# Where the two seven-product units stand in a feed-forward chunk, and when the up product of the chunk before is combined

## The reference, cut to what matters

```python
def _swiglu_ffn(x, norm_g, w_gate, w_up, w_down):
    h = _rmsnorm(x, norm_g)
    return (jax.nn.silu(h @ w_gate) * (h @ w_up)) @ w_down
# h (256, 2048) f32, w_gate and w_up (2048, 5632) f32, w_down (5632, 2048) f32
```

## Time and profile before

| | us |
|---|---|
| median of 3 runs | 2634.55 (2633.47 to 2634.83) |
| the profiled execution | 2630.96 |
| its span | 2629.2 |
| TensorE busy (modelled ends) | 2591.3 (99%) |
| VectorE busy | 1778.8 (68%) |
| ScalarE busy | 1280.2 (49%) |
| granted TensorE clock, mean | 0.999 |

### The profile page before, as it was taken

One profiled execution on the slowest core, in us unless ns is written; L12 is line 12 of the kernel. 1 busy time (PEld: TensorE's weight loads), 2 busy tenths in 40 slices (PEclk: granted clock), 3 DMA queues, 4 the chain that ended last, 5 costly groups with the idle time before them and its releaser, 6 DMA issues.

```text
span 2629.2 us, 33942 instructions
## 1 busy us (share of the span) xinstructions
PE 2591.3 (99%) x13749; PEld 2119.6 (81%) x13749; DVE 1778.8 (68%) x2085; ACT 1280.2 (49%) x1494; POOL 188.7 (7%) x346
## 2 busy tenths in 40 slices
PE   8999999999999999999999999999999999999998
PEld 7887878888888787878788888888888777888887
DVE  6887886545566796958666756555668888855444
ACT  5545454444456365546455544433555455544443
POOL 2000000000000011010001112000100000000000
PEclk9999999999999999999999999999999999999999
DMA  7666667766666665656488879644767676776554
GB/s 226 213 220 210 223 214 225 225 208 208 207 207 184 193 209 170 183 156 185 149 277 262 250 241 288 195 148 141 235 193 230 202 230 207 232 227 224 193 195 157
DMA packets 278573, 548.20 MB, mean 209 GB/s; under 512 B 25020, under 2 KB 35424, under 8 KB 278032
## 3 DMA queue, kind: packets, MB, share of 16 engines
q1 hardware_dynamic: 253904, 478.60, 57.7%
q0 software_dynamic: 24192, 66.89, 8.7%
q10 hardware_dynamic: 320, 0.53, 0.1%
HBM read 508.15 MB, written 37.77 MB: 208 GB/s over the span
## 4 chain that ended last, share of the span: by engine, by line
PE 74%; DVE 14%; DMA 5%; issue 4%; ACT 3%; POOL 0%; SPq 0%; DVEq 0%; ACTq 0%; POOLq 0%
PE pp L367 19%; PE pp L369 18%; PE pp L368 18%; PE pp L803 4%; PE pp L802 4%; PE pp L801 4%; DMA raw<-in_ffn_w_up 3%; DVE wlo L892 3%; DVE wlo L328 2%; DVE tw L900 1%; ACT whi L323 1%; DVE hid L939 1%; DVE tw L907 1%; DVE tw L904 1%; DVE cb L936 1%
## 5 line engine op out<-in xcount | busy, mean ns | idle before, releaser
L328 DVE TENSOR_TENSOR wlo<-raw,whi 128x1024 fp32r<-128x1024 f32 (+1 forms) x824 | 998.6, 1218 | 647.6 <-ACT whi L323 635.1
L323 ACT ACTIVATE whi<-raw 128x1024 fp32r<-128x1024 f32 (+1 forms) x824 | 864.9, 1054 | 950.5 <-PE pp L369 817.9
L367 PE MATMUL pp<-whi,xhi 128*128 128x512 f32 (+1 forms) x1184 | 470.3, 397 | 0.7 <-DVE xlo L504 0.7
L369 PE MATMUL pp<-wlo,xhi 128*128 128x512 f32 (+1 forms) x1184 | 459.4, 388 | 0.0
L368 PE MATMUL pp<-whi,xlo 128*128 128x512 f32 (+1 forms) x1184 | 459.3, 388 | 0.0
L801 PE MATMUL pp<-whi,xhi 128*128 128x512 f32 x832 | 323.8, 389 | 0.0
L802 PE MATMUL pp<-whi,xlo 128*128 128x512 f32 x832 | 323.8, 389 | 0.0
L803 PE MATMUL pp<-wlo,xhi 128*128 128x512 f32 x832 | 323.7, 389 | 0.0
L367 PE MATMUL pp<-whi,hhi 128*128 128x512 f32 x688 | 267.6, 389 | 0.0
L368 PE MATMUL pp<-whi,hlo 128*128 128x512 f32 x688 | 267.6, 389 | 0.0
L369 PE MATMUL pp<-wlo,hhi 128*128 128x512 f32 x688 | 267.6, 389 | 0.0
(11 more groups left out here) (498 smaller groups left out, 3199.1 us busy)
## 6 DMA issues: line engine op xcount, KB each, us to landing
raw<-in_ffn_w_gate SPq DMA_DIRECT2D x176, 512.0 KB, 4.4
raw<-in_ffn_w_up SPq DMA_DIRECT2D x176, 512.0 KB, 4.7
raw<-in_ffn_w_down SPq DMA_DIRECT2D x176, 512.0 KB, 4.5
raw<-in_w_in SPq DMA_DIRECT2D x144, 512.0 KB, 4.4
hid_dram<-hid_t POOLq DMA_DIRECT2D x43, 512.0 KB, 3.3
xq<-hid_dram POOLq DMA_DIRECT2D x156, 128.0 KB, 4.8
raw<-in_w_lift SPq DMA_DIRECT2D x32, 512.0 KB, 5.6
raw<-in_w_out SPq DMA_DIRECT2D x32, 512.0 KB, 5.1
```

The source lines that it names most:

```text
L323: nc.scalar.activation(whi[:, s, :, 0:width], raw[:, r % RING, :, 0:width], ACT.Copy).then_inc(whi_ready, 1)
L328: nc.vector.tensor_tensor(wlo[:, s, :, 0:width], raw[:, r % RING, :, 0:width], whi[:, s, :, 0:width].bitcast(F32), ALU.subtract).then_inc( ...
L367: nc.tensor.matmul(out, a_hi[:, k0 + k, tok], w_hi, start=first, stop=False)
L369: mm = nc.tensor.matmul(out, a_hi[:, k0 + k, tok], w_lo, start=False, stop=final)
```

## The change

UNIT_AFTER becomes (1, 5): unit 0 goes behind plain slot 1, unit 1 stays behind plain slot 5. The gate goes plain 0, 1, unit 0, plain 2, 3, 4, 5, unit 1, on every engine and for the loads. On VectorE finish(i - 1) is called inside unit 0, after the third sum and before the split of slot w + 1, and no longer includes the transpose; nat_turn comes behind the split of plain slot 3. Outside the seven-product chunks gated_turned keeps the old order. The rest of the diff makes the closing flags of the accumulation depend on where the last unit stands, and adds a wait for the split of the token forms, whose memory tw shares, before the first sum of the first such chunk.

```diff
-UNIT_AFTER = (3, 5)
+UNIT_AFTER = (1, 5)
...
+            unit_last = UNIT_AFTER[-1] == PLAIN - 1
...
-                        mm = product(out, xhi[:, k, tok], xlo[:, k, tok], n % RING, kk, k == 0 and opened, pr is up and k == PLAIN * SK - 1)
+                        mm = product(out, xhi[:, k, tok], xlo[:, k, tok], n % RING, kk, k == 0 and opened, k == PLAIN * SK - 1 and (pr is up or not unit_last))
...
-                product(e11, *x(1, A_FIRST), w % RING, 1, False, final).then_inc(slot_used, 1)
+                product(e11, *x(1, A_FIRST), w % RING, 1, False, final and unit_last).then_inc(slot_used, 1)
...
-                product(e21, *x(1, A_SECOND), (w + 3) % RING, 1, False, final).then_inc(slot_used, 1)
+                product(e21, *x(1, A_SECOND), (w + 3) % RING, 1, False, final and unit_last).then_inc(slot_used, 1)
...
-            def unit(w, r, u):
+            def unit(w, r, u, between=None):
...
                 dve.wait_ge(*loaded(r + 1))
+                if i == SEVEN[0] and u == 0:
+                    dve.wait_ge(sem("banks_free"), forms_split(tag))
...
                 v.tensor_tensor(tw[:, 2, :], tw[:, 0, :], blocks[:, b22, :], ALU.add).then_inc(sem("sums_ready"), 1)
+                if between is not None:
+                    between()
                 lo(w + 1, wlo[:, (w + 1) % RING, :, :], tw[:, 0:2, :], whi[:, (w + 1) % RING, :, :])
...
                 if j == 3:
-                    finish(i - 1)
+                    nat_turn(dve, None, nats[tag + "act"] + i - 1)
                 if j in UNIT_AFTER:
-                    unit(*gate["units"][UNIT_AFTER.index(j)])
+                    u = UNIT_AFTER.index(j)
+                    unit(*gate["units"][u], between=(lambda: finish(i - 1)) if u == 0 else None)
...
             op.then_inc(nat_ready, 1)
-            nat_turn(dve, None, nats[tag + "act"] + i)
...
+            def gated_turned(i):
+                gated(i)
                 nat_turn(dve, None, nats[tag + "act"] + i)
...
                         if j == 4:
-                            gated(i - 1)
+                            gated_turned(i - 1)
...
                     if c == 0 and j == 3:
-                        gated(NFC - 1)
+                        gated_turned(NFC - 1)
```

## The result

The changed kernel takes 2612.57 us (median of 4, 2609.87 to 2613.76) where the kernel before takes 2634.14 in runs beside it: 21.6 us less, ratio 0.9917, 95% interval 0.9903 to 0.9930. In a later session with more runs it was 2614.67 against 2632.74, ratio 0.9927 (0.9914 to 0.9940).

What follows compares the result with a forecast made beforehand. TensorE bounds the seven-product chunks, with 20.9 us idle; the whole loss less half a microsecond for small gaps, -20.4, takes the 2634.55 us median to 2614.2, range 2613 to 2622 (chance 0.84).

Steps and rivals of the forecast that it cites:

- The bound: Sixteen seven-product chunks: TensorE loses 20.9 us, 1.3 per chunk, in gaps at the second unit.
- The added wait, flags, e12, the transpose's way to xq: Banks wait, stop flags, TensorE product awaiting unit 0's combination, later store and reload of the hidden chunk: all cost 0.
- Unit 1: Second unit's loads get earlier-released buffers, land by 15.5 us into the chunk, bound 17.5; all gaps go, -20.9 us.
- 17.38: Latest start, in us after the chunk's first matmul, of unit 1's 7.11 us chain that opens no gap.
- Rival 1: Second unit keeps a gap, its loads taking 6.8 us beside store and reload: gain 15.3, 2619.3 us; chance 0.13.
- two signs named in the prediction: Unit 1's first sum without idle time before it; up loads' waits in ScalarE gone.
- Unit 0: First unit, wanted 5.44 us earlier: its later load lands at -1.2 to -2.2; zero gap, by 0.2 to 1.2 us.
- S: Start of unit 0's first sum against its chunk's first matmul; may be up to -0.97 without a gap.
- Rival 3: Slower: unit 0 starts on a late load with 2.70 us more work inside; 36 lost less 20.9, 2650 us; chance 0.08.
- The rule on HBM latency: Skill page's 2 us at high load would run unit 0 dry 0.8 to 1.8 us, around 2635 to 2640; rows preferred.
- a gain over 21: Sign: a gain over 21 us would mean time was lost outside the seven-product chunks, unseen by the prediction.
- transpose moved behind p3: VectorE's 1.25 us transpose moves from 5 to about 10.7 into the chunk, reload to 15.4; later reads stay covered.

Runs made afterwards that it cites:

- sum_repeated2: Changed kernel with unit 0's first sum done three times in place of once; 2638.91 us, ratio 1.0016 against the kernel before.
- turn_only: Kernel before with the block transpose alone moved, behind the split of plain slot 4, units still behind plain slots 3 and 5; 2612.64 us, ratio 0.9917.
- reload_only: Kernel before with one more wait, on GpSimd: the hidden chunk's reload starts only once plain slot 5 is split; 2616.4 us, ratio 0.9929.
- units_only: Changed kernel with the combination before unit 0, behind plain slot 1, not inside it; 2630.21 us, ratio 0.9981 against the kernel before.
- combine_only: Kernel before with the combination moved into unit 0, transpose behind slot 4's split, units still behind plain slots 3 and 5; 2620.36 us, ratio 0.9949.
- turn_inside: Changed kernel with the transpose in unit 0 too, right behind the combination; 2637.32 us, ratio 1.0008 against the kernel before.

## Why the prediction was right, and why its range was not

*The bound.* The count of 20.9 us lost in sixteen chunks, from starts, was the whole gain that there was: 20.5 came, 0.4 stayed in one chunk. The forecast took 20.4.

*The added wait, flags, e12, the transpose's way to xq.* Costed at nothing; no such wait is in the trace of the changed kernel. The ScalarE copy of the hidden chunk stood without a wait. The reload itself came later than costed, at 16.6 to 18.9 and not at 15.4, because the store before it took 4.1 to 6.2 us and not some 3. That was luck for unit 1, whose loads had landed by 17.0; what a reload at 15.4 would have cost them was not tested.

*Unit 1.* Landing expected by 15.5, at worst 17.5. The first sums came at 15.1 to 17.1 in the first profile and 15.5 to 16.8 in the second, all under 17.38. Rival 1 did not occur, though in one chunk it was 0.3 us away. The landing was sized too low: the unit's later load, costed at 4.8 us, took 4.3 to 6.2, over 4.8 in 26 of 32 chunks, with the hidden chunk's store and more weight loads beside it and no reload. So two signs named in the prediction did not come: VectorE idles before every first sum of unit 1 (0.8 to 3.0 us), and ScalarE's waits for up loads in the first block fell from 11.2 us to 5.7 and are not gone.

*Unit 0.* S expected between -2.2 and -1.2, with zero gap up to -0.97. In the two profiles it was -3.0 in three of the four chunks 1 and -2.4 to -1.0 elsewhere, but for the one -0.56. The threshold, read as the point from which the chunk gets longer, held to 0.02 us in that chunk. Rival 3's sign was right: a start 2.5 us later makes the kernel slower than before, by 0.16%. Its price was on the high side: sum_repeated2 lost 22.6 us where the same reckoning gave 28. The landing of 3.65 us was read from the loads of one stretch; in chunks 2 to 8 of the two profiles the load took 3.5 to 4.8 us.

*The rule on HBM latency.* Unit 0's later load took 3.8 us in chunk 3 (issued at 138.60, summed from 142.46). The Trainium skill, "DMA: Bandwidth & Descriptors", section "Latency and other measured facts", gives an HBM access latency of 0.2 us on average and 2 us at high load. An extra of about that size was seen beside the reload, where chunk 3's loads took 5.9 and 6.8 us against 3.5 and 4.4 with the reload held back; that this extra is HBM latency is not shown.

*Failed: the range.* The low end of 2613 was made of all 20.9 us and "half a microsecond of spread between runs". That spread term was mis-sized; the measured median is 2612.57, although the chunks gave 20.5 us and not 20.9. The kernel before ranges over 15 us in 12 runs, and medians of 4 to 6 runs of the same changed program are 2 us apart (2612.57, 2614.67). The sign was in hand: I noted that the profiled execution lay 3.6 us below the median, and took it for an offset, not for spread. A low end some 2 us lower, 2611, is an estimate from those two medians. For the same reason the 21.6 us measured first are not the sign of time lost outside the chunks that the prediction made of a gain over 21: the rest of the span was no shorter.

*Failed: what the step was for.* The prediction costed "transpose moved behind p3" at nothing and gave the 20.9 us to the second unit's new buffers. turn_only and reload_only show that moving what the transpose sets off is enough for all of it. The prediction had both facts, the 6.8 us beside the reload and 4.8 elsewhere, and even moved the reload in its timetable; it did not ask what that move is worth by itself. The unit's place and the combination inside are not needed. With the moved transpose but only one of the two, 17 of the 20.5 us are lost (units_only) or 10 (combine_only); with both and the reload beside unit 1's loads nothing is gained (turn_inside, of which 5 to 6 us are its longer chain). Whether they pay anything of themselves is not shown. The number came out since the loss was counted right and the change, by whichever part, ends at TensorE's own floor; that part of the hit is luck.

## What to carry to other kernels

When a load is late, ask first what else is being transferred at that moment and who sets that off; a wait on GpSimd was worth as much here as a new order on every engine. A transfer that is moved away slows something else, so move it beside loads that are not awaited soon. Make the timetable from one threshold, the latest start that opens no gap, and measure starts against it, since costs begin past the threshold and are not proportional. Before a range is drawn to half a microsecond, know the spread of one program against itself.

## What the runs showed of the hardware that I had not expected

Unit 1's two 512 KB loads in chunk 3 took 3.5 and 4.4 us (reload_only) or 4.1 and 4.9 (turn_only) with the reload elsewhere, and 5.9 and 6.8 (before) or 6.5 and 6.6 (turn_inside) beside the four 128 KB reloads of a transposed chunk. The reload is not the only thing that does this: in the changed kernel unit 1's up load, with the store and more weight loads beside it, took up to 6.2 us, and the second of three loads issued within 2.3 us took 5.2 in combine_only.

A gap of some 2 us was followed by a slower stretch once. In the last chunk of sum_repeated2 TensorE started nothing from 2257.78 to 2259.95 in unit 0; six starts followed within 1.3 us, then starts came 0.43 us apart in place of 0.23 for a while, with a granted clock of 0.78 over this stretch, so partly at the lower level of 1.2 GHz. The chunk lost 3.8 us where the threshold rule gives 3.0. This is TensorE there, and the stretch (start:end, length, busy, clock):

```profile
2261.59 0.63 PE L803 MATMUL pp<-whi,xshi 128*128 128x512 f32 x1
2262.02 0.63 PE L804 MATMUL pp<-whi,xslo 128*128 128x512 f32 x1
...
2264.97 0.40 PE L805 MATMUL pp<-wlo,xhi 128*128 128x512 f32 x1
```

```profile
2262.00:2268.00 6.00, 6.00 (x22) 0.78 0.90 296
```

That it is the gap that lowered the clock was not tested. In the other fifteen chunks of this profile, whose longest gap was 1.4 us, the clock stayed at the upper level.
